# An attention stage reordered around single token tiles, in a two-layer hybrid model on one core

## The reference

```python
h = h + swa_sink_attention(rms_norm(h, a_norm), w_qkv, b_qkv, sinks, w_o, cos, sin)
h = h + swiglu(rms_norm(h, f_norm), w_gate, w_up, w_down)            # 3584 wide
h = h + gated_deltanet(rms_norm(h, b_norm), ...)
h = h + moe_swiglu(rms_norm(h, m_norm), ...)                         # 8 experts, top 2
return rms_norm(h, final_norm)

def swa_sink_attention(x, w_qkv, b_qkv, sinks, w_o, cos, sin):
    q, k, v = split(x @ w_qkv + b_qkv)       # 16 heads of q, 4 of k and of v, 64 wide
    q, k = rope(q), rope(k)
    s = q @ k.T * 64 ** -0.5                 # banded: the 128 last keys, causal
    p = softmax(concat([s, sink], -1))[..., :-1]
    return (p @ v) @ w_o
```

## Time and profile before

| | us |
|---|---|
| median of 3 runs (1603.04 to 1608.95) | 1603.33 |
| the profiled execution, its time | 1603.81 |
| the profiled execution, its span | 1602.0 |

### The profile page before, as it was taken

The page is one execution under the profiler, slowest core; times in us unless marked ns, Lnnn a source line. Parts: engine busy times, 40 slices in busy tenths (PEclk is TensorE's granted clock), DMA queues, the critical chain, the costliest instruction groups (busy, mean ns, idle before and its releaser), DMA issues.

```text
span 1602.0 us, 22311 instructions
## 1 busy us (share of the span) xinstructions
PE 1522.6 (95%) x8220; PEld 1282.9 (80%) x8220; DVE 1208.7 (75%) x958; ACT 992.6 (62%) x920; POOL 136.0 (8%) x157
## 2 busy tenths in 40 slices
PE   7888999998989789999999999999999999999996
PEld 6677888877988678888888888888888888888884
DVE  6645555554675536889889888888888888888986
ACT  5444344334663434777777777777777777777773
POOL 0002000000122412920000000000000000000100
PEclk9789999998999889999999999999999999999998
DMA  9217755553332212999999999999999999999992
GB/s 369 97 38 299 255 183 195 195 185 108 116 122 80 81 40 93 342 419 401 390 377 376 382 384 369 389 379 378 384 379 380 386 370 373 395 368 366 422 388 82
DMA packets 90379, 453.96 MB, mean 283 GB/s; under 512 B 7632, under 2 KB 8032, under 8 KB 47328
## 3 DMA queue, kind: packets, MB, share of 16 engines
q1 hardware_dynamic: 83680, 430.83, 71.1%
q0 software_dynamic: 5936, 21.77, 3.4%
q10 hardware_dynamic: 720, 0.76, 0.2%
HBM read 437.60 MB, written 15.73 MB: 283 GB/s over the span
## 4 chain that ended last, share of the span: by engine, by line
PE 91%; ACT 4%; DVE 4%; issue 1%; DMA 0%; POOL 0%; POOLq 0%; SPq 0%; DVEq 0%; ACTq 0%
PE PS L304 27%; PE PS L306 27%; PE PS L305 27%; PE PS L1479 1%; DVE w_low L296 1%; ACT w_high L292 1%; PE PS L982 1%; PE PS L1313 1%; PE PS L1073 1%; PE PS L1304 0%; PE PS L1360 0%; PE PS L1049 0%; PE PS L1062 0%; ACT prob L647 0%; DMA w_raw<-in_a_w_qkv 0%
## 5 line engine op out<-in xcount | busy, mean ns | idle before, releaser
L296 DVE TENSOR_TENSOR w_low<-w_raw,w_high 128x2048 fp32r<-128x2048 f32 x407 | 932.8, 2295 | 224.7 <-ACT w_high L292 222.6
L292 ACT ACTIVATE w_high<-w_raw 128x2048 fp32r<-128x2048 f32 x407 | 779.3, 1918 | 340.9 <-PE PS L306 338.2
L304 PE MATMUL PS<-w_high,x_high 128*128 128x512 f32 x1264 | 501.5, 397 | 4.2 <-DVE x_low L1639 1.6
L306 PE MATMUL PS<-w_high,x_low 128*128 128x512 f32 x1264 | 493.8, 391 | 0.0
L305 PE MATMUL PS<-w_low,x_high 128*128 128x512 f32 x1264 | 493.1, 390 | 0.0
L304 PEld LDWEIGHTS PS<-w_high,x_high 128*128 128x128 f32 x1264 | 238.3, 188 | 54.7 <-DVE w_low L296 5.1
L306 PEld LDWEIGHTS PS<-w_high,x_low 128*128 128x128 f32 x1264 | 237.7, 188 | 50.8
L305 PEld LDWEIGHTS PS<-w_low,x_high 128*128 128x128 f32 x1264 | 238.2, 188 | 47.1
L304 PE MATMUL PS<-w_high,m_act_high 128*128 128x512 f32 x448 | 175.1, 391 | 1.6 <-DVE m_act_low L2072 1.6
L306 PE MATMUL PS<-w_high,m_act_low 128*128 128x512 f32 x448 | 174.4, 389 | 0.0
L305 PE MATMUL PS<-w_low,m_act_high 128*128 128x512 f32 x448 | 174.4, 389 | 0.0
(11 more groups left out here) (295 smaller groups left out, 1271.4 us busy)
## 6 DMA issues: line engine op xcount, KB each, us to landing
w_raw<-in_m_w_blocks SPq DMA_DIRECT2D x336, 1024.0 KB, 7.1
w_raw<-in_b_w_in SPq DMA_DIRECT2D x16, 1024.0 KB, 5.4
w_raw<-in_f_w_gate SPq DMA_DIRECT2D x14, 1024.0 KB, 5.1
w_raw<-in_f_w_up SPq DMA_DIRECT2D x14, 1024.0 KB, 5.1
w_raw<-in_f_w_down SPq DMA_DIRECT2D x14, 1024.0 KB, 4.7
w_raw<-in_a_w_qkv SPq DMA_DIRECT2D x6, 1024.0 KB, 12.7
x_slots_dram<-zeros POOLq DMA_DIRECT2D x12, 512.0 KB, 7.4
w_raw<-in_a_w_o SPq DMA_DIRECT2D x4, 1024.0 KB, 14.3
```

What stands on the lines that cost most here:

```text
L292: nc.scalar.activation(WH[:, n % SPLIT, :], W[:, n % RAW, :], ACT.Copy).then_inc(hi_done, 1)
L296: nc.vector.tensor_tensor(WL[:, n % SPLIT, :], W[:, n % RAW, :], WH[:, n % SPLIT, :].bitcast(f32), ALU.subtract).then_inc(lo_done, 1)
L304: nc.tensor.matmul(o, sH, mH, start=first, stop=False)
L306: return nc.tensor.matmul(o, sL, mH, start=False, stop=last)
```

## The change

The attention stage is written anew, and the norm behind it.

- **qkv pieces.** Column block 2 (k, v) comes first, then 0, then 1. The last one, i = 2, is computed tile by tile (`qkv_piece(2, half, t, 0)`), 12 matmuls at a time between the steps of the heads. Its pieces, and those of the output projection, are used twice, once for each tile.
- **Order of the eight steps.** `ITEMS`: groups 0 and 1 of both tiles, then groups 2 and 3.
- **Mask.** A matmul of an identity with the mask (`eyeR`, `maskR`, fp32r), two for each step, writes the mask into PSUM, and the scores accumulate on it; the factor 1/8 is put on q when it is evicted. DVE reduces the maximum from PSUM (`maxima`), and ACT reads its `Exp` from PSUM.
- **Row sums.** The values get a 65th column of ones (`vals`), so the sum comes out of `values`; the accumulators of `Exp` go. The sink's `Exp` is an instruction with semaphores of its own.
- **Rope** works on one tile at a time, with a signed sine table: one addition instead of a subtraction and an addition.
- **Output projection in halves.** Half 0 (heads of groups 0 and 1) is multiplied and added to h between the later steps; half 1 follows the last step. There are twice as many additions to h.
- **Norm by tile.** Squares, 1/rms, scaling (now with the gain, `f_gain`, broadcast over the partitions by one more transfer on POOL's queue, behind a wait), transposes and splits go tile by tile, and the first gate piece too (`first_gate`).

```diff
+                for i, cb in enumerate((2, 0, 1)):
+                    for half in range(2):
+                        fetch(sp, base["att"] + 2 * i + half, 0, "cols", col_src(a_w_qkv[0], cb, half))
+                        if (i, half) == (1, 0):
+                            sp.dma_start(cst[:, 128:], consts[:, 128:]).then_inc(sem("cst_in"), 16)
+                for half in range(2):
+                    for cb in range(2):
+                        fetch(sp, base["att"] + 6 + 2 * half + cb, 0, "cols", col_src(a_w_o[0], cb, half))
...
+                    pool.wait_ge(lo_done, base["att"] + 4)
+                    pool.dma_start(f_gain[:], f_norm[0].partition_broadcast(128)).then_inc(loaded_att, 16)
...
+                    act.wait_ge(sem("qkT_ps"), 2 * i + t + 1)
+                    b = (8, 0, 4)[i]
+                    nc.scalar.activation(qkT[:, b:b + 4, 128 * t:128 * t + 128], PS[:, bank, :].rearrange("p (b c) -> p b c", b=4),
+                                         ACT.Copy, scale=1.0 if i == 0 else AD ** -0.5).then_inc(sem("qkT_done"), 1)
...
+                        last = nc.scalar.activation(prob[:, a % 2, hh, 0:nk], PS[:, 2 + 2 * (a % 2) + hh % 2, hh // 2 * nk:hh // 2 * nk + nk],
+                                                    ACT.Exp, bias=negm[:, a, hh:hh + 1])
...
+                small_high()
+                act.wait_ge(sem("ident_in"), 16)
+                nc.scalar.activation(eyeR[:], ident, ACT.Copy)
+                act.wait_ge(sem("cst_in"), 16)
+                nc.scalar.activation(maskR[:], over_heads(C("att"), 2), ACT.Copy).then_inc(sem("mask_in"), 1)
+                for n in range(3, 6):
+                    split_high(act, n0 + n)
+                evict_qk(0, 0, 4)
+                evict_qk(0, 1, 5)
+                split_high(act, n0 + 6)
+                evict_qk(1, 0, 6)
+                evict_qk(1, 1, 7)
+                exps(0)
+                exps(1)
+                sink_exp(0)
+                sink_exp(1)
+                probs_out(0)
+                probs_out(1)
+                evict_qk(2, 0, 7)
+                exps(2)
+                sink_exp(2)
+                exps(3)
+                sink_exp(3)
+                split_high(act, n0 + 7)
+                probs_out(2)
+                split_high(act, n0 + 8)
+                probs_out(3)
+                o_high(0, 0)
+                exps(4)
+                evict_qk(2, 1, 7)
+                exps(5)
+                sink_exp(4)
+                sink_exp(5)
+                probs_out(4)
+                probs_out(5)
+                exps(6)
+                sink_exp(6)
+                o_high(0, 1)
+                probs_out(6)
+                exps(7)
+                sink_exp(7)
                 split_high(act, n0 + 9)
+                split_high(act, f0)
+                probs_out(7)
+                o_high(1, 0)
+                o_high(1, 1)
+                norm_tile("ffn", 0)
+                split_high(act, f0 + 1)
+                turn_tile("ffn", 0)
+                norm_tile("ffn", 1)
+                split_high(act, f0 + 2)
+                turn_tile("ffn", 1)
+                split_high(act, f0 + 3)
 
...
+                def qkv_piece(i, half, t, bank):
+                    n = n0 + 2 * i + half
+                    pe.wait_ge(lo_done, n + 1)
+                    wh, wl = high_low(n, 4)
+                    for kk in range(4):
+                        k = 4 * half + kk
+                        if i == 0 and t == 0:
+                            x_ready("att", k)
+                        last = mm3(PS[:, bank, :], xH[:, k, 128 * t:128 * t + 128], xL[:, k, 128 * t:128 * t + 128],
+                                   wh[:, kk], wl[:, kk], k == 0, k == KD - 1)
+                    if t == 1:
+                        last.then_inc(w_used, 1)
+                    elif half == 1:
+                        last.then_inc(sem("piece_ps"), 1)
+
...
+                                         start=True, stop=False, skip_group_check=True)
                     for hh in range(AG):
                         hd = AG * g + hh
                         r = slice(64 * (hd % 2), 64 * (hd % 2) + 64)
...
+                        last = nc.tensor.matmul(PS[:, b0 + hh % 2, col:col + nk],
                                                 qkT[r, hd // 2, 128 * t:128 * t + 128], qkT[r, 8 + g, 0:nk],
-                                                start=True, stop=True)
+                                                start=False, stop=True, skip_group_check=True)
                     last.then_inc(sem("score_ps"), 1)
...
-                                                    qkv[:, kt, 1280 + 64 * g:1280 + 64 * g + 64],
-                                                    start=(kt == 0), stop=(kt == t))
...
+                def turn_o(half, t):
+                    pe.wait_ge(sem("o_att_done"), 4 * half + 2 * t + 2)
+                    for kk in range(4):
+                        k = 4 * half + kk
+                        last = nc.tensor.transpose(PS[:, 0, 128 * kk:128 * kk + 128], o_att[:, t, 128 * k:128 * k + 128], ident)
+                    last.then_inc(sem("tile_ps"), 1)
+
+                def out_piece(half, t, cb, bank):
+                    n = n0 + 6 + 2 * half + cb
+                    pe.wait_ge(lo_done, n + 1)
+                    pe.wait_ge(sem("tile_low"), 2 * half + t + 1)
+                    wh, wl = high_low(n, 4)
+                    for kk in range(4):
+                        k = 4 * half + kk
+                        last = mm3(PS[:, bank, :], xH[:, k, 128 * t:128 * t + 128], xL[:, k, 128 * t:128 * t + 128],
+                                   wh[:, kk], wl[:, kk], kk == 0, kk == 3)
+                    last.then_inc(w_used if t else sem("piece_ps"), 1)
+
+                for half in range(2):
+                    for t in range(TT):
+                        qkv_piece(0, half, t, t)
+                for half in range(2):
+                    for t in range(TT):
+                        qkv_piece(1, half, t, 2 + t)
+                turn_qk(0, 0, 4)
+                turn_qk(0, 1, 5)
+                pe.wait_ge(sem("piece_read"), 1)
+                qkv_piece(2, 0, 0, 0)
+                turn_qk(1, 0, 6)
+                turn_qk(1, 1, 7)
+                pe.wait_ge(sem("mask_in"), 1)
+                pe.wait_ge(sem("piece_read"), 4)
                 scores(0)
                 scores(1)
-                for a in range(8):
-                    turn_probs(a)
-                    if a + 2 < 8:
-                        pe.wait_ge(sem("masked"), a + 1)
-                        scores(a + 2)
-                    values(a)
-                turn("att_o", o_att, sem("o_att_done"), 8)
-                for cb in range(2):
-                    tokens_by_columns("att_o", n0 + 6 + 2 * cb, 2 * cb, cb)
+                qkv_piece(2, 1, 0, 0)
+                turn_probs(0)
+                scores(2)
+                turn_probs(1)
+                scores(3)
+                turn_qk(2, 0, 7)
+                values(0)
+                pe.wait_ge(sem("piece_read"), 5)
+                qkv_piece(2, 0, 1, 0)
+                qkv_piece(2, 1, 1, 0)
+                turn_probs(2)
+                values(1)
+                scores(4)
+                turn_probs(3)
+                scores(5)
+                pe.wait_ge(sem("piece_read"), 6)
+                turn_o(0, 0)
+                values(2)
+                pe.wait_ge(sem("probT_done"), 4)
+                turn_qk(2, 1, 7)
+                out_piece(0, 0, 0, 0)
+                turn_probs(4)
+                scores(6)
+                turn_probs(5)
+                values(3)
+                pe.wait_ge(sem("piece_read"), 7)
+                out_piece(0, 0, 1, 0)
+                scores(7)
+                pe.wait_ge(sem("piece_read"), 8)
+                turn_o(0, 1)
+                values(4)
+                turn_probs(6)
+                out_piece(0, 1, 0, 0)
+                values(5)
+                pe.wait_ge(sem("piece_read"), 9)
+                out_piece(0, 1, 1, 0)
+                turn_probs(7)
+                values(6)
+                pe.wait_ge(sem("piece_read"), 10)
+                turn_o(1, 0)
+                values(7)
+                out_piece(1, 0, 0, 2)
+                turn_o(1, 1)
+                out_piece(1, 0, 1, 3)
+                out_piece(1, 1, 0, 4)
+                out_piece(1, 1, 1, 5)
...
+                def first_gate(half, t):
+                    pe.wait_ge(lo_done, n0 + half + 1)
+                    pe.wait_ge(sem("tile_low"), 2 * TILE_NO["ffn", t] + half + 1)
+                    wh, wl = high_low(n0 + half, 4)
+                    for kk in range(4):
+                        k = 4 * half + kk
+                        last = mm3(PS[:, t, :], xH[:, k, 128 * t:128 * t + 128], xL[:, k, 128 * t:128 * t + 128],
+                                   wh[:, kk], wl[:, kk], k == 0, k == KD - 1)
+                    if t:
```

(181 more changed lines are left out.)

206 lines of the change are left out of this document (87 added, 119 removed).

## The result

The changed kernel takes 1578.03 us (median of 4 runs, 1577.72 to 1578.64) against 1604.42 of the kernel before beside it; the ratio is 0.9839, with a 95% interval of 0.9822 to 0.9855. The forecast was 1579.5. The profiled execution took 1578.32, against 1603.81: 25.5 us less. One execution of the kernel before, of 8606.19 us beside the last group of kernels, was in a slow state and stands outside every comparison. Where the result differs from kernel to kernel by less than some 2 us, the times alone can't tell, and the traces are read at a fixed point instead.

The account below looks back on a forecast made before the run. PE was taken as the bound: 129.66 - 100.2 (work) - 3.8 (waits) - 1.7 (clock) = 24.0 us gained, so 1603.81 gives 1579.8, the median 1579.3, taken as 1579.5; range 1574 to 1590.

Parts of the forecast that it names:

- The stretch on PE: From PE's first dense matmul to the first gate pair's end: 129.66 us before, new floor 100.2, 24.0 gained.
- Small operations: Heads' steps on PE: transposes of probabilities 6.2 us, scores 7.5, values 12.4, added mask matmuls 2.7.
- The four waits: PE waits: ACT's last eviction 0.4, division of step 6 0.7, copies after tile 0's transposes 1.2, tile 1's scaling 1.5 us.
- The clock: One fall of PE's clock near the values or the norm's waits, charged 1.7 us, bounds nothing and 5.0.
- Rival 1: Heads' steps: late ACT or DVE exposes chains between PE's blocks, eight times 1.0 to 1.5; 1588 to 1592; chance 0.14.
- PE has 2.72 us or more queued, so I find no wait: Interleaved heads' steps: other steps' work or 2.72 us of a piece covers DVE and ACT; no wait from 41 to 88.
- Rivals 2 and 3: Interleaved part: clock falls repeatedly, 10.6 us more, 1590, chance 0.12; or PE stays at 1.2 GHz, up to 1639, chance 0.04.
- Rival 4: Experts' stretch or an early feed-forward piece does not move with PE, gain given back, about 1603 us; chance 0.05.

Follow-up runs that it names:

- blocks: Changed kernel with nothing between the heads' steps: all qkv pieces first, then the eight steps alone, then all output pieces; 1601.05 us, ratio 0.9989.

## Why the prediction was right, point by point

- *The stretch on PE.* Forecast 100.2 + 3.8 + 1.7 = 105.7 us from the first dense matmul to the end of the first gate pair, and 24.0 gained. Measured: 14.70 to 120.2, 105.5, and 24.0 gained at the first point that can be compared. (The 118.5 that the prediction names for this end leaves its 1.7 us for the clock out; with them it is 120.2.) The medians gained more, 26.4, and the forecast time is 1.5 too high. Of the 2.4 beyond 24.0, 1.5 came from the later stages (1.6 of the span, the clock ahead of the delta net), which the sum did not have, and 0.9 is the spread of executions: the median before lies 0.6 above the profiled one (the forecast had it 0.5 below), the median after 0.3 below.
- *Small operations.* I had taken 28.8 us for probabilities, scores, values and mask; by the chain they are 5.7 + 6.8 + 10.6 + 3.3 = 26.4. The values were mis-sized most, 12.4: I used a group's length (2.00 in the earlier trace rows), which includes the tail of its last matmul, though the next group begins 1.83 after it. The mask costs 3.3 rather than 2.7: a pair of narrow ones took 0.47 and 0.43 in the first two steps and 0.29 and 0.23 in the later ones (forecast 0.23), a wide pair 0.47 (0.45).
- *What the 2.4 us went to.* I had not counted the changes between groups. The 56 transposes of q, k, the result and the normed tiles took 6.8 instead of 6.1: four of them took 0.44 in some places and 0.58 or 0.59 in others. The first dense matmul behind a small group took 0.43 or 0.44 twice, as in the rows above, and 0.23 to 0.29 in eight other places:

```profile
66.92 0.24 PE PS L309
73.97 0.29 PE PS L309
```

  These ten are 0.7 us over the plain step. The remaining 0.8 or so are spread over the dense matmuls, and no run takes them apart. Two errors cancel here, by luck.
- *The four waits.* Forecast 0.4, 0.7, 1.2 and 1.5, sum 3.8. Measured 0.3, 0.6, 1.1 and 1.8, sum 3.8.
- *The clock.* I charged 1.7 for one fall near the values or the norm. It did not fall there. In the profiled execution the first nine dense matmuls ran at half speed instead, 3.93 us from the start of the first to that of the tenth (14.70 to 18.63), against 2.13 in the kernel before (14.53 to 16.66): 1.8 us; in the trace before and three others they did not. The size was right for the wrong place, by chance.
- *Rival 1* (the lists catch each other) did not come true, but it was nearer than the 0.14 suggests. The step "PE has 2.72 us or more queued, so I find no wait" is right for this amount of dense work only: with 8.2 us less of it, or the mask back on DVE, the waits are there at once. PE and the chain on DVE are within a few microseconds of each other.
- *Rivals 2 and 3* (the clock among small operations): the windows show 1.00 throughout. In the kernel with less dense work the clock fell once idle time came to the small operations, which did not make it fall by themselves. By the rule cited from the Trainium skill ("TensorE: Matmul & The Clock Gate", section "A second HAM failure mode: psum-queue depth-cycling") the clock might have swung with the cycling through bank 0; this trace does not show it, at 1.00 from 36.50 to 97.60.
- *Rival 4* (given back behind): no; the gapless stretches are as long as before.
- *Where the gain is.* Interleaving 22.5 us (blocks against the changed kernel), norm by tile 5.2. Either is measured with everything else in place, so they don't add up to 26. The mask by matmul is worth 2 to 4 in the bare chain and nothing once it is covered; the row sums and the rope were not taken apart.

## What to carry to other kernels

When one engine has the long dense work and the others a chain of short steps, put the dense work between the steps in pieces a few microseconds long; it covers the waits and keeps the clock up at once, and here that was most of the gain. Count each engine's list to the same end, since cover works until the chain is the longer one, and then less dense work on PE no longer helps: the waits come back, and with them the low clock. Take the length of a short group from its start to the next one's start, and leave some time for the changes between groups.

## What the runs showed of the hardware

- POOL's 128 x 1 `tensor_scalar` took 0.19 us with DVE idle, and 1.96 when it started 0.37 us into DVE's 2.28 us subtraction of two SBUF operands; it ended 0.05 us behind that. Moving the subtraction brought back 0.19. The Trainium skill, "GPSIMD Engine Reference", section "Specifications", says that the two engines share their SBUF interface and contend when DVE reads two SBUF inputs, or when it runs in a 2-port mode; the runs agree, and show a wait for the rest of DVE's instruction. DVE's scaling in the kernel before has one SBUF tensor only, and held POOL in the same way: 0.70 us, to 0.05 behind its end.

```profile
126.73 0.75 DVE L1605 TENSOR_SCALAR xs<-h,rstd 128x1024 f32<-128x1024 f32 x1 [1.61 <-POOL rstd L417]
126.83 0.70 POOL L416 TENSOR_SCALAR ms<-ss 128x1 f32<-128x1 f32 x1 [0.20 <-ACT xs L603]
```

- In nine of thirteen traces the first dense matmuls step by 0.43 us, the step at 1.2 GHz, and the trace has no clock record until they step by 0.23; a window over such a stretch reads 1.00.
- One idle stretch of 2.4 us brought the clock to 0.50 (in the window 110 to 111); waits of 1.1 and 1.8 us with a piece of dense work between them did not. The longest wait alone does not decide it: in the kernel with less dense work it fell after waits of 1.4, 1.3 and 0.9 us within some 11 us, with small operations and short pieces between them.
